# Differential attention, steps 1 to 3: one dense step issued between the scores and the transposes that follow them

## The chip, the cores and the metric

The kernel runs on one core of a Trainium2 chip. The metric is the device time of one execution in microseconds. A core has five engines that run their own instruction queues in order and meet only at semaphores: TensorE (PE, with its weight loads shown apart as PEld), VectorE (DVE), ScalarE (ACT), GpSimd (POOL), and SyncE (SP), which here issues the transfers.

## The reference, cut to what matters

The kernel computes two transformer blocks on a sequence of 1024 positions and a width of 1024, in float32. The part that the change touches is the differential attention of the second block. Eight heads, each with two maps of scores, are computed in blocks of 128 queries:

```
def diff_attention(q, k, v, g_q, g_k, lam, g_sub, lambda_init):
    qn = head_rmsnorm(q, g_q) * (HEAD_DIM_2 ** -0.5)
    kn = head_rmsnorm(k, g_k)
...
        s = jnp.einsum('bqhid,bkhid->bihqk', qblk, kn)
        s = jnp.where(allowed, s + bias, neg)
        p = jax.nn.softmax(s, axis=-1)
        a = p[:, 0] - lam * p[:, 1]
        return jnp.einsum('bhqk,bkhe->bqhe', a, vf)
...
    o = head_rmsnorm(o, g_sub) * (1.0 - lambda_init)
```

Before it, q, k and v of a head come from a product of the normalised input with a slice of w_in (z = h @ w_in). `allowed` lets a query see keys up to the end of its own chunk of 64.

## The kernel before, in words

Every dense product is made to float32 accuracy from two halves: an operand is split into a high part (HH for the activations, WH for the weights) and the remainder (HL, WL), and three products are summed in PSUM. A chunk is 128 output rows of such a product. It has eight **dense steps**, one for each 128 rows of the contraction; a step (`step`, which calls `mm3`, line 545 in the rows) is six matmuls of 512 columns, each with a weight load of 128 columns. ScalarE rounds the weights of a chunk to WH, GpSimd makes WL, and SP loads the next chunk's weights once WL is done.

The attention has eight heads j. The heads 1 to 6 run in a loop that holds two heads in its body, one for each parity of the buffers; head 0 and head 7 are written out. A head has eight **steps s** = 0 to 7, one for each block of 128 queries, and step s has s + 1 blocks of 128 keys. I call the stretch of TensorE's program that begins with scores(s) slot s. In slot s TensorE issues, in this order:

- `scores(s)` (line 885): the scores of both maps, into two pairs of PSUM banks. It waits until VectorE has read the scores of step s - 1 (`d_max`).
- `turn(s - 1, 0)` (line 866): the transposes of the weighted difference dP of step s - 1, up to four blocks, and from five blocks on `turn(s - 1, 1)` for the rest. It waits for dP (`d_a`) and until the bank with the blocks turned before has been emptied (`d_atl`).
- in slot 0 the transposes of the values (line 837), in slot 2 `output_sums` (line 844), the sums of squares of the outputs of the head before (not in head 0), in slots 4 and 6 `group_sums` (line 829), the same for the next head's q and k.
- `steps(n)`: dense steps of the next head's q, k and v, three chunks, 24 steps in all. They fill TensorE while the other engines work on the softmax. `D_STEPS = (0, 3, 3, 2, 3, 5, 3, 5)` says how many a slot has, and the larger half of them (`early`; none of them in slots 4 and 6) stands before the second group of transposes and the values. The first step of each chunk waits for `free[0]`, until the accumulator (the first two PSUM banks) is free; for a head's first dense step that is when VectorE has made dVL, the low part of the values, from it. Head 7 has no next head and no dense steps of this kind.
- `values(s - 1)` (line 661) for odd s - 1: the product of the turned differences of two steps with the values.

The other engines follow step by step. **VectorE**: two passes over the scores of step s (line 1702) add the bias, write the negated scores and find the row's minimum; then it makes the low part ATL of the turned blocks of step s - 1 (line 1395); then it waits for both exponentials, and lines 1754 to 1756 and 1391 make dP of step s. In slot 1 it makes dVL ahead of its passes; at the end of slot 2 it copies the output of two steps (line 1731) and normalises the outputs of the head before (dOT, line 1388). **ScalarE**: the high part ATH of the turned blocks of step s - 1 (line 1286), then the two exponentials of step s (lines 1304 and 1306) with their sums; in slot 2, between the two, `ln_outputs` (line 1246), the logarithm of the sums of squares that output_sums has made, and after the exponentials line 1255. Ln and exp each come with a load of their function table.

Of the kernel before, what the change touches and what calls it, by code (L numbers as in the profile page):

```python
# [121 lines left out]
def blocks_of(t, g):  # L122

    return range(4 * g, min(t + 1, 4 * g + 4))
# [23 lines left out]
def group_index(s):  # L148

    return NG * (s // ST) + (GROUPS[s % ST - 1] if s % ST else 0)  # L150


def block_kernel(nc, xt, cb, vecs, consts, mods, wst, out):
    with ExitStack() as ctx:
# [385 lines left out]
        def _(pe):  # L540
# [8 lines left out]
            def step(c, slot, pair, RH, RL, k, nk=KT, read=None):  # L549

                if k == 0:
                    pe.wait_ge(w_hi, c + 1)
                    pe.wait_ge(w_lo, c + 1)
                b = slice(k * P, (k + 1) * P)
                last = mm3(pair * S, WH[slot][:, b], WL[slot][:, b], RH, RL, k, k == 0, k == nk - 1)
                if k == nk - 1:
                    last.then_inc(chunk_done, 1)
                elif read is not None:
                    last.then_inc(read, 1)
# [92 lines left out]
            def value_sum(t, n, VH, VL):  # L652


                h, l = ATH[n], ATL[n]
                parts = [(kb, v, a) for kb in (0, t, *range(1, t)) for v, a in ((VH, h), (VH, l), (VL, h))]
                if t == 1:
                    parts = [parts[i] for i in (0, 3, 4, 5, 1, 2)]
                for i, (kb, v, a) in enumerate(parts):
                    r = 1 if kb == t else 0  # L660
                    last = pe.matmul(PS[:, OB + (2 * n + r) * P:OB + (2 * n + 2) * P], v[:, kb * P:(kb + 1) * P],
                                     a[:, (2 * kb + r) * P:(2 * kb + 2) * P], start=(i == 0), stop=(i == len(parts) - 1))
                return last

            def next_chunk(c, slot, name, k):

                if k == 0:
                    pe.wait_ge(free[0], USED["bout" if name == "y" else name][0])
                pe.wait_ge(f_lo, FILL[name] + k + 1)
                step(c, slot, 0, HH, HL, k)  # L670
# [129 lines left out]
            for g in (2, 3):  # L800
                s = (C_POOL + g) % 2
# [23 lines left out]
            def group_sums(n):  # L825

                pe.wait_ge(d_sq, n)
                for h in (0, HALF):
                    last = pe.matmul(PS[:, h:h + HALF], dBD[:, :], dSQ[:, h:h + HALF], start=True, stop=True)  # L829
                last.then_inc(d_ss, 1)  # L830

            def turn_values(j, par):

                pe.wait_ge(d_v, j + 1)
                for t in range(ST):
                    b = slice(t * P, (t + 1) * P)
                    last = pe.transpose(PS[:, b], dVR[par][:, b], IDF[:, :])
                last.then_inc(d_vt, 1)

            def output_sums(n):  # L840

                pe.wait_ge(d_sq, n)
                for h, o in enumerate(OSUM):
                    last = pe.matmul(PS[:, o:o + HALF], ONES[:, :], dSQ[:, h * HALF:(h + 1) * HALF], start=True, stop=True)
                last.then_inc(d_ss, 1)
# [8 lines left out]
            def attention_d(j, par, fill=True, first=False):  # L854


                used = 3 * j + (ud[0] + 2)

                def turn(s, g):
                    if s < 0 and first or g >= len(GROUP_BLOCKS[s % ST]):  # L860
                        return
                    pe.wait_ge(d_a, ST * j + (s + 1))
                    if not (first and s == 0 and g == 0):
                        pe.wait_ge(d_atl, NG * j + (group_index(s) + g))
                    for n, kb in enumerate(blocks_of(s % ST, g)):
                        last = pe.transpose(PS[:, TB + n * P:TB + (n + 1) * P], dP0[s % 2][:, kb * P:(kb + 1) * P], IDF[:, :])
                    last.then_inc(d_t, 1)

                def scores(s):
                    n = (s + 1) * P  # L870
                    q = slice(s * P, (s + 1) * P)
                    pe.wait_ge(free[1], ST * j + (ud[1] + s))
                    if s == 4 and not first:
                        pe.wait_ge(d_lo, j)
                    if first and s == 0:
                        pe.wait_ge(free[2], ud[2])
                    else:
                        pe.wait_ge(d_max, ST * j + s)
                    parts = ((dQH, dKH), (dQH, dKL), (dQL, dKH))
                    for i, (l, rr) in enumerate(parts):  # L880
                        for c0 in range(0, n, HALF):
                            w = min(HALF, n - c0)
                            for m in range(2):
                                rows, base = slice(m * HD, (m + 1) * HD), (1 + m) * S
                                last = pe.matmul(PS[:, base + c0:base + c0 + w], l[par][rows, q], rr[par][rows, c0:c0 + w],
                                                 start=i == 0, stop=i == 2)
                                if i == 2 and c0 + w == n:
                                    last.then_inc(d_s, 1)

                def values(s):  # L890

                    if s % 2 == 0 or s < 0 and first:
                        return
                    if not (first and s < 4):
                        pe.wait_ge(d_o, ST // 2 * j + (s + 1) // 2 - 2)
                    if s == 1:
                        pe.wait_ge(free[0], used + 1)
                    pe.wait_ge(d_atl, NG * j + group_index(s + 1))
                    v = par if s >= 0 else 1 - par
                    value_sum(s % ST, s // 2 % 2, dVH[v], dVL[v]).then_inc(d_av, 1)  # L900

                k = 0

                def steps(n):

                    nonlocal k
                    for _ in range(n if fill else 0):
                        c = k // KT
                        if k % KT == 0:
                            pe.wait_ge(free[0], used + (1 + c))  # L910
                        step(3 * j + (C_QKV2 + 3 + c), (C_QKV2 + 3 * par + 3 + c) % 2, 0, HH, HL, k % KT)
                        k += 1

                pe.wait_ge(d_split, j + 1)
                for s in range(ST):
                    scores(s)
                    turn(s - 1, 0)
                    if s == 0:
                        turn_values(j, par)
                    if s == 2 and not first:  # L920
                        output_sums(3 * j + 2)
                    if fill and s in (4, 6):
                        group_sums(3 * j + (3 if s == 4 else 4))
                    early = 0 if s in (4, 6) else (D_STEPS[s] + 1) // 2
                    steps(early)
                    if not fill and s >= 3:
                        next_chunk(C_AB, C_AB % 2, "ab", s - 3)
                    turn(s - 1, 1)
                    values(s - 1)
                    steps(D_STEPS[s] - early)  # L930
                if fill:
                    return
                turn(ST - 1, 0)
                next_chunk(C_AB, C_AB % 2, "ab", ST - 3)
                turn(ST - 1, 1)
                next_chunk(C_AB, C_AB % 2, "ab", ST - 2)
                values(ST - 1)
                pe.wait_ge(d_max, ST * KT)
                output_sums(3 * KT)

            attention_d(0, 0, first=True)
            with pe.Fori(0, (KT - 2) // 2) as i:
                for m in range(2):
                    attention_d(2 * i + (1 + m), 1 - m)
            attention_d(KT - 1, 1, fill=False)
            next_chunk(C_AB, C_AB % 2, "ab", KT - 1)
            u = USED["ab"]
# [1041 lines left out]
```

## Time and profile before

| | |
|---|---|
| time, median of 3 runs | 3137.21 us (3136.54 to 3137.8) |
| the profiled execution's own time | 3134.09 us |
| its span, first to last instruction | 3132.3 us |
| TensorE busy | 2847.5 us (91%) |
| VectorE, ScalarE, GpSimd busy | 1257.9, 1129.1, 720.7 us |
| granted clock of TensorE, mean | 0.964 of full speed |
| where the differential attention lies | 1684 to 2226 us of the span |

Busy times of different engines overlap; they don't add up to the span. The busy time of TensorE counts matmuls, which are pipelined: the end of one lies behind the start of the next. So what a piece of TensorE's work takes is read from start to start. A row of the time order gives the start, the duration, the engine, the line and the tiles (out<-in), how many instructions are merged in it, and in brackets how long the engine had been idle and what released it.

### The profile page before, as it was taken

To read this page: it belongs to the slowest core of one execution; us is meant where nothing else is said; L and a number is where in the kernel's file an instruction comes from. 1 tells how busy PE (TensorE), PEld (TensorE's weight loads), DVE (VectorE), ACT (ScalarE), POOL (GpSimd) and SP (SyncE) were. 2 spreads that over 40 slices of the span, in tenths; PEclk is the share of its full clock that TensorE was granted. 3 is DMA by queue.
4 is the path that set the end of the run, shared out by engine and by line. 5 is a ranking of instruction groups with operands and counts; after the bars stand their busy time and mean duration, and the time that the engine had idled before them with its cause. 6 is when DMAs were issued, how large, how long until landed. Compare 5 with 4: busy or idle time off the path is not lost.

```text
span 3132.3 us, 38031 instructions
## 1 busy us (share of the span) xinstructions
PE 2847.5 (91%) x13672; PEld 2283.7 (73%) x13672; DVE 1257.9 (40%) x1751; ACT 1129.1 (36%) x1585; POOL 720.7 (23%) x387
## 2 busy tenths in 40 slices
PE   5999998998888875979998898898798999999999
PEld 3888886877777764768786666665586888888887
DVE  5545433135666654370103555556442412112121
ACT  4212213225565553243215666666312312112120
POOL 0222221223444431212222111110112122222222
PEclk8999998999999986989999999998899999999999
DMA  5433322442211211102231000001331111111112
GB/s 198 133 122 115 120 68 71 170 158 78 85 57 47 86 48 45 63 32 96 101 134 37 33 29 27 34 33 55 114 114 47 41 47 47 54 47 47 47 48 100
DMA packets 62570, 236.81 MB, mean 76 GB/s; under 512 B 6944, under 2 KB 7584, under 8 KB 59936
## 3 DMA queue, kind: packets, MB, share of 16 engines
q1 hardware_dynamic: 62496, 235.88, 21.7%
q8 instruction: 40, 0.66, 0.1%
q14 instruction: 34, 0.28, 0.0%
HBM read 191.81 MB, written 44.04 MB: 75 GB/s over the span
## 4 chain that ended last, share of the span: by engine, by line
issue 69%; PE 17%; POOL 8%; DVE 4%; ACT 2%; POOLq 0%; DVEq 0%; ACTq 0%; DMA 0%; SPq 0%
PE PS L545 10%; POOL WL L1825 7%; DVE bC L1580 2%; PE PS L706 2%; PE PS L728 2%; DVE ATL L1395 2%; ACT PS L1117 1%; PE PS L691 1%; PE PS L754 1%; POOL dBIAS L1880 1%; PE PS L711 0%; ACT bB L1116 0%; PE PS L829 0%; POOLq L1872 0%; ACT ATH L1109 0%
## 5 line engine op out<-in xcount | busy, mean ns | idle before, releaser
L1825 POOL TENSOR_TENSOR WL<-WR,WH 128x1024 fp32r<-128x1024 f32 x215 | 522.0, 2428 | 2096.0 <-ACT WH L984 2090.0
L545 PE MATMUL PS<-HH,WH 128*128 128x512 f32 x2272 | 727.2, 402 | 93.7 <-issue 28.8
L545 PE MATMUL PS<-HL,WH 128*128 128x512 f32 x2272 | 713.1, 396 | 0.0
L545 PE MATMUL PS<-HH,WL 128*128 128x512 f32 x2272 | 711.3, 395 | 0.0
L545 PEld LDWEIGHTS PS<-HH,WH 128*128 128x128 f32 x2272 | 426.5, 192 | 199.1 <-issue 74.2
L545 PEld LDWEIGHTS PS<-HL,WH 128*128 128x128 f32 x2272 | 435.6, 192 | 93.5
L545 PEld LDWEIGHTS PS<-HH,WL 128*128 128x128 f32 x2272 | 434.3, 191 | 92.9
L984 ACT ACTIVATE WH<-WR 128x1024 fp32r<-128x1024 f32 x214 | 225.6, 1054 | 590.5 <-PE PS L545 413.7
L545 PE MATMUL PS<-GH,WH 128*128 128x512 f32 x768 | 236.7, 389 | 1.6 <-DVE TMP L1795 1.5
L545 PE MATMUL PS<-GH,WL 128*128 128x512 f32 x768 | 236.5, 389 | 0.0
L545 PE MATMUL PS<-GL,WH 128*128 128x512 f32 x768 | 236.4, 389 | 0.0
L1580 DVE TENSOR_TENSOR_SCAN bC<-PS,EPSC 128x256 f32<-128x256 f32 (+7 forms) x128 | 172.9, 1352 | 102.5 <-ACT PS L1117 102.3
L1853 POOL TENSOR_TENSOR bB<-bB,bC 128x256 f32<-128x256 f32 (+7 forms) x128 | 154.0, 1205 | 176.9 <-DVE bC L1580 175.8
L1395 DVE TENSOR_TENSOR ATL<-PS,ATH 128x512 fp32r<-128x512 f32 (+3 forms) x288 | 152.6, 546 | 49.2 <-ACT ATH L1286 24.7
L545 PEld LDWEIGHTS PS<-GH,WH 128*128 128x128 f32 x768 | 144.0, 188 | 32.2 <-issue 1.9
L545 PEld LDWEIGHTS PS<-GH,WL 128*128 128x128 f32 x768 | 144.2, 188 | 29.9
L545 PEld LDWEIGHTS PS<-GL,WH 128*128 128x128 f32 x768 | 144.2, 188 | 29.9
L1817 DVE TENSOR_TENSOR X<-PS,X 128x1024 f32 x32 | 39.2, 1225 | 292.2 <-PE PS L545 292.2
L691 PE MATMUL PS<-IDF,bB 128*128 128x128 f32 x576 | 99.0, 298 | 58.3 <-DVE ATL L1395 57.5
L691 PEld LDWEIGHTS PS<-IDF,bB 128*128 128x128 f32 x576 | 67.2, 148 | 82.8 <-DVE ATL L1395 52.9
L1808 DVE SCALAR_TENSOR_TENSOR TMP<-PS,TMP 128x1024 f32<-128x1024 f32 x32 | 39.2, 1224 | 207.7 <-ACT TMP L1374 207.7
L1374 ACT ACTIVATE TMP<-PS 128x1024 f32<-128x1024 f32 x32 | 32.9, 1027 | 233.4 <-PE PS L545 233.4
(226 smaller groups left out, 3504.7 us busy)
## 6 DMA issues: line engine op xcount, KB each, us to landing
WR<-wst SPq DMA_DIRECT2D x215, 512.0 KB, 3.4
TMP<-mods SPq DMA_DIRECT2D x48, 512.0 KB, 3.7
MRAW<-mods SPq DMA_DIRECT2D x16, 512.0 KB, 10.5
v_hl<-VS SPq DMA_DIRECT2D x8, 1024.0 KB, 6.3
bV<-v_hl SPq DMA_DIRECT2D x8, 1024.0 KB, 7.4
X<-xt SPq DMA_DIRECT2D x4, 1024.0 KB, 8.0
x_b<-X SPq DMA_DIRECT2D x8, 512.0 KB, 4.8
k_hi<-KSH SPq DMA_DIRECT2D x8, 512.0 KB, 4.9
```

Source lines behind the costliest of these rows:

```text
L545: last = pe.matmul(PS[:, dst0 + q:dst0 + q + HALF], l, rr[:, k * S + q:k * S + q + HALF], start=a, stop=z)
L691: last = pe.transpose(PS[:, base + n * P:base + (n + 1) * P], bB[t % 2][h][:, kb * P:(kb + 1) * P], IDF[:, :])
L706: pe.matmul(PS[:, base + c0:base + c0 + w], l[par][rows, q], rr[par][rows, c0:c0 + w], start=i == 0, stop=i == 2 and c0 + w < n)
L728: last = pe.matmul(PS[:, o + r * P:o + 2 * P], value_weights(V, kb, h), a[:, (2 * kb + r) * P:(2 * kb + 2) * P], start=i == 0 and a is ATH ...
L984: act.activation(WH[slot][:, :], WR0[:, :], ACT.Identity).then_inc(w_hi, 1)
L1374: act.activation(T[m], PAIR[s], ACT.Relu).then_inc(ff_r, 1)
L1395: return dve.tensor_tensor(dst, value, high.bitcast(F32), ALU.subtract)
L1580: dve.tensor_tensor_scan(bC[h][:, S - n:S][:, ::-1], c, EPSC[:, 0:1].broadcast_to([P, n]), 1.0, ALU.mult, ALU.bypass).then_inc(free[1 + h], 1)
L1808: dve.scalar_tensor_tensor(out=T[2 + m], in0=PAIR[s], scalar=0.0, in1=T[m], op0=ALU.max, op1=ALU.mult).then_inc(free[s], 1)
L1817: dve.tensor_tensor(x, PAIR[s], x, ALU.add).then_inc(free[s], 1)
L1825: pool.tensor_tensor(WL[slot][:, :], WR0[:, :], WH[slot][:, :].bitcast(F32), ALU.subtract).then_inc(w_lo, 1)
L1853: pool.tensor_tensor(b, b, bC[h][:, S - n + 1:S + 1], ALU.mult).then_inc(b_a, 1)
```

## The change

In slots 1, 2 and 3 of every head one dense step is issued after the scores and ahead of the transposes, and one less after them. The number of dense steps in a slot and their order stay the same. In head 7 `steps` issues nothing, and there is no change.

```
                 for s in range(ST):
                     scores(s)
+                    if s in (1, 2, 3):
+                        steps(1)
                     turn(s - 1, 0)
...
                     early = 0 if s in (4, 6) else (D_STEPS[s] + 1) // 2
-                    steps(early)
+                    steps(early - (1 if s in (1, 2, 3) else 0))
```

With `early` of 2, 2 and 1 in these slots: slot 1 goes from scores, turn(0), 2 dense steps, 1 dense step to scores, 1 dense step, turn(0), 1, 1. Slot 2 goes from scores, turn(1), output_sums, 2 dense steps, values(1), 1 dense step to scores, 1 dense step, turn(1), output_sums, 1, values(1), 1. Slot 3 goes from scores, turn(2), 1 dense step, 1 dense step to scores, 1 dense step, turn(2), 1.

## Rows read from the trace of the kernel before

**Rows 1.** The page, part 1: busy time of TensorE.
```profile
PE 2847.5 (91%) x13672; PEld 2283.7 (73%) x13672; DVE 1257.9 (40%) x1751; ACT 1129.1 (36%) x1585; POOL 720.7 (23%) x387
```

**Rows 2.** Waits of TensorE, 1752 to 2152 us: total us, times, longest us.
```profile
PE PS L866 <- DVE dP L1391: 9.3, 6, 1.6
PE PS L545 <- DVE dVL L1395: 6.1, 6, 1.0
```

**Rows 3.** Busy time by stretch: from:to, length, busy by engine, granted clock, DMA.
```profile
1688.60:1692.50 3.90, 3.90 (x10) 3.04 (x11) 2.07 (x9) 1.09 (x4) 2.10 (x1) 0.58 0.16 47
1754.00:2150.00 396.00, 357.38 (x1932) 267.13 (x1931) 226.65 (x543) 255.03 (x399) 57.63 (x24) 1.00 0.10 33
```

**Rows 4.** In order of time, TensorE, head 4: start us, duration us, what.
```profile
1960.26 0.33 PE L866 MATMUL PS<-IDF,dP 128*128 128x128 f32 x1
1961.61 0.70 PE L545 MATMUL PS<-HH,WH 128*128 128x512 f32 x2 [1.02 <-DVE dVL L1395]
...
1965.88 0.44 PE L885 MATMUL PS<-dKH,dQH 64*128 64x384 f32 x2
...
1966.60 0.44 PE L866 MATMUL PS<-IDF,dP 128*128 128x128 f32 x2
1966.87 1.88 PE L844 MATMUL PS<-dSQ,ONES 128*128 128x512 f32 x4
...
1973.51 0.50 PE L885 MATMUL PS<-dKH,dQH 64*128 64x512 f32 x2
...
1974.40 0.55 PE L866 MATMUL PS<-IDF,dP 128*128 128x128 f32 x3
...
1977.63 0.56 PE L885 MATMUL PS<-dKH,dQH 64*128 64x512 f32 x4
...
1980.43 0.65 PE L866 MATMUL PS<-IDF,dP 128*128 128x128 f32 x4 [1.55 <-DVE dP L1391]
```

**Rows 5.** In order of time, ScalarE and VectorE, head 4.
```profile
1962.10 0.51 ACT L1304 ACTIVATE dP<-dP,SM 128x256 f32<-128x256 f32 x1 [0.53 <-DVE SM L1702]
...
1964.07 0.48 DVE L1391 SCALAR_TENSOR_TENSOR dP<-dP,SM,dP 128x256 f32<-128x256 f32 x1
...
1967.07 0.38 ACT L1286 ACTIVATE ATH<-PS 128x256 fp32r<-128x256 f32 x1 [3.88 <-PE PS L866]
...
1967.47 1.28 ACT L1246 ACT_TABLE_LOAD   x1
...
1968.79 1.27 ACT L1246 ACTIVATE dSQ<-PS,EPSC 128x512 f32<-128x512 f32 x2
...
1970.08 1.28 ACT L1304 ACT_TABLE_LOAD   x1
...
1971.37 0.62 ACT L1304 ACTIVATE dP<-dP,SM 128x384 f32<-128x384 f32 x1
...
1973.62 0.62 DVE L1391 SCALAR_TENSOR_TENSOR dP<-dP,SM,dP 128x384 f32<-128x384 f32 x1
...
1974.49 1.28 DVE L1388 SCALAR_TENSOR_TENSOR dOT<-dOT,GS,dRS 128x1024 f32<-128x1024 f32 x1
...
1975.69 0.69 DVE L1702 CUSTOM_DVE_ANT_0 dP<-PS,dBIAS 128x512 f32<-128x512 f32 x1
...
1977.03 0.72 ACT L1304 ACTIVATE dP<-dP,SM 128x512 f32<-128x512 f32 x1 [1.55 <-DVE SM L1702]
...
1979.55 0.75 DVE L1391 SCALAR_TENSOR_TENSOR dP<-dP,SM,dP 128x512 f32<-128x512 f32 x1
```

**Rows 6.** In order of time, TensorE and ScalarE, head 0.
```profile
1688.60 0.73 PE L545 MATMUL PS<-HH,WH 128*128 128x512 f32 x2 [1.06 <-DVE dVL L1395]
...
1694.51 0.44 PE L885 MATMUL PS<-dKH,dQH 64*128 64x384 f32 x2
...
1702.83 0.72 ACT L1304 ACTIVATE dP<-dP,SM 128x512 f32<-128x512 f32 x1 [0.41 <-DVE SM L1702]
...
1706.17 0.65 PE L866 MATMUL PS<-IDF,dP 128*128 128x128 f32 x4 [0.34 <-DVE dP L1391]
```

More of the change, by code:

```diff
@@ L916, in attention_d @@
                     scores(s)
+                    if s in (1, 2, 3):
+                        steps(1)
                     turn(s - 1, 0)
@@ L924, in attention_d @@
                     early = 0 if s in (4, 6) else (D_STEPS[s] + 1) // 2
-                    steps(early)
+                    steps(early - (1 if s in (1, 2, 3) else 0))
                     if not fill and s >= 3:
```

## The prediction, made before the changed kernel was run

> **What bounds the kernel now.** Read the page first. TensorE is busy for 2847.5 us of the span of 3132.3 us [rows 1], so the end of the kernel is set by TensorE's work and by the holes in it, and an edit that only reorders that work can pay or cost only through the holes. Read next the waits of TensorE over the six middle heads of the differential attention (heads 1 to 6, 1752 to 2152 us). Two lines matter to this change: 9.3 us in six waits ahead of the transposes of step 3 (line 866, for the weighted difference dP of line 1391), and 6.1 us in six waits ahead of a head's first dense step (line 545, for dVL, which frees the accumulator) [rows 2]. Six heads, six equal waits: the heads repeat one pattern, so one head can be read for all. The granted clock over them is 1.00, the 2.4 GHz level; the stretch of head 0 in which its first dense steps run is at 0.58, a mixture of the two levels [rows 3].
>
> Third, read head 4 in order of time. I write turn(n) for the transposes that TensorE makes of step n's dP, and scores(n) for its score matmuls. In the row order of TensorE [rows 4], turn(0) starts at 1960.26, TensorE then idles 1.02 us for dVL, three dense steps run from 1961.61 to scores(2) at 1965.88, turn(1) follows at 1966.60 and output_sums at 1966.87; scores(3) at 1973.51, turn(2) at 1974.40, scores(4) at 1977.63, and then TensorE stands until turn(3) at 1980.43, the wait of 1.55 us of rows 2.
>
> What ends that last wait is found by walking back on ScalarE and VectorE [rows 5]. dP of step 3 (1979.55, 0.75 us) follows exp(3) at 1977.03; that waited for the minimum of step 3, whose passes over the scores start on VectorE at 1975.69; they stand behind the normalisation of dOT (1974.49, 1.28 us), that behind dP of step 2 (1973.62), that behind exp(2) at 1971.37. Ahead of exp(2) ScalarE has a table load, the two Ln passes (1968.79) and another table load (1967.47), and ahead of these the eviction ATH of turn(1), at 1967.07, before which ScalarE idled 3.88 us for turn(1) itself. From turn(1) to turn(3) there is thus one unbroken chain through ScalarE and VectorE, 1980.43 - 1966.60 = 13.83 us, none of whose links waits for dense work. TensorE has less than that to do in the meantime, which is the 1.55 us hole.
>
> **The change part by part.** Nothing is added or removed: 24 dense steps a head, in the same order, with the same waits inside them. The moved step's six matmuls and six weight loads and its waits (for the accumulator at step 0 of a chunk, for w_hi and w_lo) are all on TensorE; no DMA moves. SP's load of the next weights and the split on GpSimd hang on chunk_done, and the eighth dense step, which sets it, stays the last of slot 3; neither queue is passed by anything. One step now stands ahead of turn(0), turn(1) and turn(2) in heads 0 to 6; head 7 has no dense steps.
>
> The price of a step: three of them fill 1961.61 to 1965.88, 4.27 / 3 = 1.42 us each. At the lower clock of head 0 the same three fill 1688.60 to 1694.51 [rows 6], 5.91 / 3 = 1.97 us each. The ends for a step are thus 1.42 and 1.97; in the six heads at clock 1.00 I take 1.42.
>
> Slot 1, turn(0). The moved step is the head's first, the one that waits for dVL. It can't start before 1961.61 wherever it stands, so the hole stays, and turn(0), which ran inside it, is now queued behind the wait: 1961.61 + 1.42 = 1963.0 instead of 1960.26. Behind turn(0) wait its eviction and then exp(1) on ScalarE (1962.10 before, now about 1963.6) and dP of step 1 on VectorE (end 1964.07 + 0.48 = 1964.6, now 1966.1). Who waits for that dP is turn(1), which comes after 1968, so this lateness is covered by 2 us of TensorE's own work; without that cover it would cost 1.5 us a head. What does show is that turn(0) leaves the cover of the wait. Between nothing and its own 0.33 us, I take half of what the two transposes of turn(1) hold TensorE (1966.60 to 1966.87, 0.27), 0.13 us.
>
> Slot 2, turn(1). A step of 1.42 us goes between scores(2) and turn(1), whose dP is ready. Turn(1) moves by 1.42 + 0.13 = 1.55 us, to 1968.15, and output_sums, queued behind it, moves with it. This is the head of the chain above, and ScalarE was idle there. Every link moves by 1.55: dP of step 2 ends at about 1975.8, the passes of step 3 start at 1977.2, exp(3) at 1978.6, turn(3) at 1980.43 + 1.55 = 1981.98.
>
> The Trainium skill bears on the length of this chain. Rows 5 show a table load of 1.28 us both ahead of Ln and ahead of the exp that follows. "ScalarE: Activation LUTs", section "Table sets: the hidden batching unit", says that one set, natural_log_exp_and_others, holds both functions and that ln followed by exp needs one load. By that page the chain could be two loads shorter, the wait of 1.55 us would be mostly gone before the change, and the change would then cost only some 0.5 us a head, about 3141 us in all. The trace doesn't agree, this program does switch tables each time, and the measurement decides.
>
> Slot 3, turn(2). Scores(3) starts at 1973.6, ends its work in about 0.9 us (1973.51 to 1974.40), and the moved step fills 1974.5 to 1975.9, just as long as dP of step 2 is late. So turn(2) goes at about 1975.9 without a wait of its own; its eviction is over by 1977, before exp(3) needs ScalarE at 1978.6. This edit costs nothing, because slot 2's delay covers it; alone it would push the eviction to about 1976.9, still ahead of exp(3) at 1977.03. One step is left in slot 3, and TensorE reaches scores(4) at about 1977.7. There a new wait stands: scores(4) needs both passes of step 3 done, which was so at 1977.0 and now is so at about 1978.6. That is about 1.0 us of hole, and after scores(4) another of 2.0 us ahead of turn(3) where there were 1.55.
>
> From turn(3) on all three engines are late by the same 1.55 us, and the rest of the head is unchanged, so nothing gives it back. The six heads cost 6 x 1.55 = 9.3 us.
>
> Head 0 has no output_sums, no Ln pair and no dOT normalisation in slot 2. Its exp(3) waited 0.41 us after the eviction of turn(2), and turn(3) followed after a hole of 0.34 [rows 6]. Turn(2) moves by 1.55, the eviction with it, exp(3) by 1.55 - 0.41 = 1.1, and turn(3) by 1.1. Ends for head 0: 0 and 2.1 (a step at the lower clock). Sum: 9.3 + 1.1 = 10.4 us. The profiled execution took 3134.1 us (span 3132.3), so it would take 3144.5. It lies 3.1 us below the median of the runs, and I put the sum on the median: 3137.2 + 10.4 = 3147.6 us.
>
> **Rivals.** (1) Not slower. If turn(1) were not what releases ScalarE (if the load and the Ln were waiting for something of their own that ends 1.5 us after turn(1)), the chain would stay where it is and only TensorE's own small terms count: 7 x 0.13 us for turn(0) uncovered, less about 0.1 us a head of the 0.36 us that turn(2) waited. That is nothing: 3137.2 us. It decides from the point where ScalarE has 1.55 us of slack behind turn(1). For it: turn(1) and output_sums stand so close that the row of the Ln alone doesn't tell which it followed. Against it: both move together, and ScalarE's row shows 3.88 us idle up to turn(1) and then no gap to exp(2).
>
> (2) The clock falls. Each head gets 1.5 us more of holes within 6 us, and if the granted clock then fell once a head to 1.2 GHz as in head 0's first steps, where holes of about 1 us came shortly before, each head would pay 5.91 - 4.27 = 1.64 us more: 6 x 1.64 = 9.8, so 3157.4 us. Against it: the same heads hold holes of 1.0 and 1.55 us now and keep 1.00 throughout [rows 2, 3]. The Trainium skill, "TensorE: Matmul & The Clock Gate", section "HAM oscillation — how this bites in real kernels", says that waits between bursts of matmuls put the clock back, burst after burst. By that rule this rival would be right; the trace so far agrees only for head 0.
>
> (3) Faster. The step stands in for waits: the 0.36 us ahead of turn(2) vanishes six times and nothing else moves, which gives 3135.0 us. To be faster by more than a measurement tells, the 1.55 us ahead of turn(3) would have to go too, and no moved step stands between scores(4) and turn(3).
>
> **How the numbers follow.** A measurement of this kernel can tell about 0.2%, 6.3 us. Chances: the forecast (3145 to 3150) 0.68; part of the shift only, in some heads or with slack that I don't see (3140 to 3145) 0.07; the clock rival, wholly or in some heads (3150 to 3157.4) 0.10; not slower 0.12; faster 0.03, of which most lies within 0.2%. Slower by over 0.2%, from 3143.5 up: 0.68 + 0.10 + 0.04 = 0.82; within 0.2%: 0.16; faster by over 0.2%: 0.02. The range takes in the forecast, the partial case and the lower half of the clock rival: 3140 to 3154 us.
>
> **What would show it.** In the trace of the changed kernel, over heads 1 to 6: head to head about 1.55 us more; ScalarE's idle time before the eviction of turn(1) longer, about 3.9 us or more, and from there to exp(2) the same 4.3 us; a new line of waits of scores on the passes of line 1702, six of about 1 us; the six waits ahead of turn(3) near 2.0 us; the 1.0 us wait for dVL unchanged; clock 1.00. Turn(3) coming 13.8 us after turn(1) as before is the test of the chain. I am wrong if that distance shrinks to about 12.3 us (rival 1), or if the granted clock of these heads is below 1.00 (rival 2).

## The result, and the profile after

The changed kernel takes 3158.1 us (median; 3157.3 to 3159.8) against 3136.9 us before in the same comparison: slower by 21.3 us, ratio 1.0071 with a 95% interval of 1.0057 to 1.0086. The profiled execution took 3159.8 us, its span 3158.0, that is 25.7 us over the span of before. The prediction was 3147.6 us, range 3140 to 3154. The direction was right, the size half of what came.

Start with the page of the changed kernel, part 1, the row that answers to [rows 1]:

```profile
PE 2866.2 (91%) x13672; PEld 2298.5 (73%) x13672; DVE 1257.5 (40%) x1751; ACT 1129.0 (36%) x1585; POOL 719.3 (23%) x387
```

The number of matmuls is the same, and TensorE is busy 18.7 us longer with them. A step that only waits would leave the busy time alone; so part of the loss isn't waiting but slower matmuls. The other engines are busy as long as before.

The waits of TensorE over heads 1 to 6 of the changed kernel, 1750 to 2170 us (total us, times, longest us), beside [rows 2]:

```profile
PE PS L866 <- DVE dP L1393: 12.8, 6, 2.1
...
PE PS L545 <- DVE dVL L1397: 7.2, 6, 1.3
PE PS L885 <- DVE SM L1704: 3.9, 6, 0.6
```

The six waits ahead of turn(3) went from 1.55 to 2.1 us, and a new line of six appeared, scores(4) for the passes of step 3, 0.65 us each. Together they are 3.9 + 12.8 - 9.3 = 7.4 us more. The wait for dVL was 1.0 and is 1.28 in most heads, because turn(0) no longer stands inside it. That is another 1.1 us over the six heads, and not unchanged as the prediction had it.

Now one head in order of time, TensorE and ScalarE, head 4 of the changed kernel. Its rows answer to [rows 4, 5]:

```profile
1973.20 0.70 PE L545 MATMUL PS<-HH,WH 128*128 128x512 f32 x2 [1.28 <-DVE dVL L1397]
...
1979.84 0.38 PE L866 MATMUL PS<-IDF,dP 128*128 128x128 f32 x2
1980.06 1.88 PE L844 MATMUL PS<-dSQ,ONES 128*128 128x512 f32 x4
1980.26 0.38 ACT L1288 ACTIVATE ATH<-PS 128x256 fp32r<-128x256 f32 x1 [3.96 <-PE PS L866]
...
1984.56 0.62 ACT L1306 ACTIVATE dP<-dP,SM 128x384 f32<-128x384 f32 x1
...
1987.71 0.49 PE L866 MATMUL PS<-IDF,dP 128*128 128x128 f32 x3
...
1990.22 0.72 ACT L1306 ACTIVATE dP<-dP,SM 128x512 f32<-128x512 f32 x1 [1.49 <-DVE SM L1704]
1990.24 0.56 PE L885 MATMUL PS<-dKH,dQH 64*128 64x512 f32 x4 [0.65 <-DVE SM L1704]
...
1993.62 0.65 PE L866 MATMUL PS<-IDF,dP 128*128 128x128 f32 x4 [2.14 <-DVE dP L1393]
```

From the first dense step to turn(1) it is 1979.84 - 1973.20 = 6.64 us, 1.65 more than the 4.99 of before. ScalarE idles 3.96 us up to turn(1), exp(2) follows the eviction by 4.30 us as before, and from turn(1) to turn(3) it is 13.78 us against 13.83. The chain is the one described, unchanged in length and only started later.

The turn(3) of heads 1 to 6 in the changed kernel, and then those of the kernel before (that of head 4 stands in [rows 4]), give the length of a head:

```profile
1778.12 0.65 PE L866 MATMUL PS<-IDF,dP 128*128 128x128 f32 x4 [2.14 <-DVE dP L1393]
1850.26 0.65 PE L866 MATMUL PS<-IDF,dP 128*128 128x128 f32 x4 [2.13 <-DVE dP L1393]
1924.15 0.66 PE L866 MATMUL PS<-IDF,dP 128*128 128x128 f32 x4 [2.14 <-DVE dP L1393]
1993.62 0.65 PE L866 MATMUL PS<-IDF,dP 128*128 128x128 f32 x4 [2.14 <-DVE dP L1393]
2067.41 1.11 PE L866 MATMUL PS<-IDF,dP 128*128 128x128 f32 x4 [2.14 <-DVE dP L1393]
2140.64 0.65 PE L866 MATMUL PS<-IDF,dP 128*128 128x128 f32 x4 [2.14 <-DVE dP L1393]
```

```profile
1775.99 0.65 PE L866 MATMUL PS<-IDF,dP 128*128 128x128 f32 x4 [1.55 <-DVE dP L1391]
1843.89 0.65 PE L866 MATMUL PS<-IDF,dP 128*128 128x128 f32 x4 [1.55 <-DVE dP L1391]
1912.58 0.65 PE L866 MATMUL PS<-IDF,dP 128*128 128x128 f32 x4 [1.55 <-DVE dP L1391]
...
2049.08 0.65 PE L866 MATMUL PS<-IDF,dP 128*128 128x128 f32 x4 [1.56 <-DVE dP L1391]
2116.93 0.65 PE L866 MATMUL PS<-IDF,dP 128*128 128x128 f32 x4 [1.55 <-DVE dP L1391]
```

Before, heads take 67.9 and 68.7 us in turn (the loop's body holds two). After, they take 72.1, 73.9, 69.5, 73.8 and 73.2. The third of these is longer by 1.6 us, which is the chain. The others are longer by 4.2 to 5.4 us. What is different about them is the clock. Stretches of the changed kernel (from:to, length, busy by engine, granted clock, DMA), beside [rows 3]:

```profile
1754.00:2170.00 416.00, 369.43 (x1909) 276.91 (x1908) 223.10 (x535) 253.62 (x398) 58.91 (x24) 0.95 0.09 31
1779.00:1782.40 3.40, 3.40 (x11) 2.03 (x9) 1.35 (x3) 2.77 (x3) 3.32 (x2) 0.57 0.00 0
1895.00:1902.00 7.00, 5.54 (x26) 5.35 (x26) 1.75 (x6) 3.21 (x7) 2.37 (x1) 0.54 0.04 8
1904.00:1973.00 69.00, 61.11 (x332) 45.58 (x331) 38.96 (x93) 43.86 (x69) 9.85 (x4) 1.00 0.07 23
```

The mean clock of these heads fell from 1.00 to 0.95. The 1.2 GHz level is granted in nine stretches: right after turn(3) in heads 1, 2, 4, 5 and 6 (the second row is the first of them), and in slot 0 of heads 2, 3, 5 and 6 (the third row). Between the dense steps of head 3 and those of head 4, the last row, there is none, and that is the head that is only 1.6 us longer.

So the 25.7 us divide as follows, from first dense step to turn(3) and from there to the next head's first dense step. The chain: 6 x 1.6 = 9.6 us, and 1.05 in head 0 (17.57 us from the first to the second before, 18.62 after). The clock: 2.6, 3.6, 0.0, 3.6 and 3.8 us between heads, and 2.0 from turn(3) of head 6 to the end of the span (1.3 of it by turn(1) of head 7), 15.6 us. One fall that the kernel before had in slot 0 of head 1 is gone, 2.0 us back, and the profiled execution reached head 0 1.4 us later, which is ahead of the first changed instruction. These are two single executions. The medians lie 21.3 us apart; if the chain costs the same 10.6 us in every execution, 10.7 us are left for the clock.

### The profile page after: what moved, and what is told of

The parts are those of the page before. It is cut to its first block, busy times and chain, and to the rows that moved or that the text cites. A ratio compares the mean times of both kernels' runs of the same rounds, so it can differ in the third digit from the quotient of the medians.

```text
span 3158.0 us, 38031 instructions
## 1 busy us (share of the span) xinstructions
PE 2866.2 (91%) x13672; PEld 2298.5 (73%) x13672; DVE 1257.5 (40%) x1751; ACT 1129.0 (36%) x1585; POOL 719.3 (23%) x387
## 4 chain that ended last, share of the span: by engine, by line
issue 66%; PE 19%; POOL 7%; DVE 4%; ACT 2%; POOLq 0%; DVEq 0%; ACTq 0%; DMA 0%; SPq 0%
PE PS L545 13%; POOL WL L1827 6%; DVE bC L1582 2%; PE PS L706 2%; PE PS L728 2%; DVE ATL L1397 2%; ACT PS L1119 1%; PE PS L691 1%; PE PS L754 1%; POOL dBIAS L1882 1%; PE PS L711 0%; ACT bB L1118 0%; PE PS L598 0%; PE PS L829 0%; ACT ATH L1111 0%
```

## The experiments

Two causes had to be told apart and shown: which of the moved steps starts the chain, and what makes the clock fall. For the clock there were two theories. By the one, it falls after the longer holes around scores(4). By the other, holes that were there all along (those of slot 0 among them) make it fall or not according to when they come, and in longer heads they come at other times. Both can be true together. The runs below stand in that order. Each ratio is against runs of the kernel before on the same chip.

**One slot at a time.** Slot 2 alone:

```
-                    if s in (1, 2, 3):
+                    if s in (2,):
                         steps(1)
...
-                    steps(early - (1 if s in (1, 2, 3) else 0))
+                    steps(early - (1 if s in (2,) else 0))
```

> The step is moved ahead of the transposes in slot 2 alone. Chain theory (turn(1) releases the chain through ScalarE and VectorE that ends in turn(3)): turn(3) comes about 1.4 us later in each of heads 1 to 6, the distance from turn(1) to turn(3) stays 13.8 us, and the time rises by about 6 x 1.4 = 8.5 us plus 1 us in head 0, to about 3146 us if the clock stays at its upper level in these heads, and by some 10 us more, to about 3157 us, if the clock falls as it does in the changed kernel. Rival (the three moved steps share the cost): a third of the 21 us, about 3144 us. Rival (turn(1) has slack): 3137 us.

Measured: 3148.75 us, ratio 1.0043 (1.0027 to 1.0060), 13.4 us more. The mean clock of heads 1 to 6 is 0.98, with five falls, three in slot 0 (of heads 1, 3 and 6) and two after turn(3). Its waits of TensorE over the six heads:

```profile
PE PS L866 <- DVE dP L1393: 17.1, 12, 1.7
```

Twelve waits for dP, not six: turn(2) now waits too, 1.2 us, since its dP is late and no step has been moved ahead of it. From first dense step to turn(3) it is 20.3 us against 18.8, in each of the six heads; the head without a fall is 1.5 us longer. One moved step makes the whole chain late, at 6 x 1.45 = 8.7 us. In head 0, where 1 us was expected, nothing changed (17.62 us against 17.57). The rest of the 13.4 us is lower clock, less of it than in the changed kernel, so the number lies between the 3146 and the 3157 of the chain theory.

Slots 1 and 3, `if s in (1, 3)` in both places:

> The step is moved in slots 1 and 3 and left where it was in slot 2. Chain theory: turn(1) comes only 0.13 us later, exp(3) still waits for the passes on VectorE, so 6 x 0.1 = under 1 us in the six heads, and 0 to 1 us in head 0, where exp(3) follows turn(2) more closely: 3137 to 3139 us, clock 1.00 in heads 1 to 6. Rival (each moved step costs): two thirds of the 21 us, about 3151 us.

Measured: 3136.3 us, ratio 1.0005 (0.9995 to 1.0014), no change in the median. Six waits ahead of turn(3) of 1.49 us, clock:

```profile
1754.00:2145.00 391.00, 351.39 (x1897) 262.34 (x1897) 222.70 (x536) 253.19 (x398) 58.14 (x24) 1.00 0.10 33
```

So the chain's cost in the six heads comes with the step of slot 2. The other two add 0.15 us a head, and the 1.05 us of head 0 is theirs: its hole ahead of turn(3) is 1.18 us here and stayed at 0.34 with slot 2 alone. Together that is 8.7 + 0.9 + 1.0 = 10.6 us, the chain's part of the changed kernel.

The clock's part is not settled by these two. The changed kernel costs 8 us more than slot 2 alone, and the ten executions of slots 1 and 3 fall in two groups: five of 3130.7 to 3133.8 us at a mean clock of 0.965 to 0.966, the profiled one among them, and five of 3138.7 to 3140.7 us at 0.961 to 0.963. The same program keeps the clock up in one execution and loses some of it in another; no trace shows where it was lost in the second group.

**Take the Ln out of the chain.** In this run and the next, output_sums is issued in slot 1, after turn(0), and ScalarE takes the logarithm after the exponentials of step 1. On the kernel before:

```
-                    if s == 2 and not first:
+                    if s == 1 and not first:
                         output_sums(3 * j + 2)
...
-                    if s == 2 and not first:
-                        ln_outputs(3 * j + 2)
...
+                    if s == 1 and not first:
+                        ln_outputs(3 * j + 2)
                     if s == 2 and not first:
                         exp_d(3 * j + 2, d_lo, j)
```

> The kernel before, but output_sums is issued in slot 1 right after turn(0), where TensorE waits for dVL, and ScalarE takes the logarithm after the exponentials of step 1, where it is idle for 3.9 us until turn(1). Chain theory: the two table loads and the Ln passes leave the chain from turn(1) to turn(3), exp(3) is then released by the scores of step 3, and the hole ahead of turn(3) shrinks from 1.55 to about 0.5 us: 6 x 1.1 = 6.5 us less, about 3129 us with the clock as before. If the length of a head decides whether the holes of slot 0 lower the clock, heads that are 1.1 us shorter can lose it again: up to 6 x 1.5 = 9 us on top. If the chain does not run through the Ln, 3136 us as before.

Measured: 3131.2 us, ratio 0.9987 (0.9978 to 0.9997), 4.5 us less. Waits of TensorE over the six heads:

```profile
PE PS L844 <- ACT dSQ L1316: 5.3, 6, 0.9
PE PS L866 <- DVE dP L1391: 3.8, 6, 0.6
```

The hole ahead of turn(3) fell from 1.55 to 0.64 us, close to the 0.5 expected, and from turn(1) to turn(3) it is 11.24 us (1969.01 to 1980.25 in head 4), 2.6 less than before. Output_sums now waits 0.9 us for the squares, and the wait for dVL is gone from the list. Every second head also has one fall of the clock in slot 0, where before only one head had. A head without one is 0.7 us shorter, one with it 0.7 us longer.

The same on the changed kernel:

> The changed kernel with output_sums and the logarithm in slot 1 as in the run before. Chain theory: a late turn(1) no longer delays turn(3) through the Ln; what is left is that turn(2) is a step late and exp(3) then follows it, about 1.1 us a head against the run before, so a hole of about 1.6 us ahead of turn(3) as in the kernel before, and 3131 to 3137 us at a clock of 1.00, up to 9 us more if the clock falls in slot 0. If the moved steps cost by themselves and not by the Ln chain, 3150 us or more.

Measured: 3142.2 us, ratio 1.0020 (1.0010 to 1.0030). That is 16 us under the 3158 of the changed kernel (from another chip, but the kernel before took the same there, 3136.9 and 3135.7). But it is still 11.0 us over the run before, which has the same base without the moved steps: moving the pair makes both kernels faster and takes about half of the change's cost, not all of it. A head without a fall is 68.6 us long, where the run before has 67.15: 1.4 us more for the moved steps, hardly less than the 1.6 us with the pair in the chain.

The expectation had the mechanism wrong here. It let exp(3) hang on the late turn(2). The trace of head 4 shows otherwise:

```profile
1973.33 0.38 PE L866 MATMUL PS<-IDF,dP 128*128 128x128 f32 x2
...
1975.44 0.61 ACT L1304 ACTIVATE dP<-dP,SM 128x384 f32<-128x384 f32 x1
...
1980.01 0.49 ACT L1288 ACTIVATE ATH<-PS 128x384 fp32r<-128x384 f32 x1 [2.31 <-PE PS L866]
...
1981.10 0.72 ACT L1304 ACTIVATE dP<-dP,SM 128x512 f32<-128x512 f32 x1 [0.60 <-DVE SM L1704]
...
1984.51 0.66 PE L866 MATMUL PS<-IDF,dP 128*128 128x128 f32 x4 [1.97 <-DVE dP L1393]
```

The eviction of turn(2) (1980.01) is over 0.60 us before exp(3), which is released by VectorE's passes, as in the run before (0.63 us there). Turn(3) follows turn(1) by 11.18 us, against 11.24 in the run before. It is the old chain from turn(1), through one table load and exp(2), with the Ln pair out of it and 2.6 us shorter, and a late turn(1) still makes all of it late. The Ln pair made the chain long; the change doesn't need it to cost. The medians' 11 us don't divide further: the profiled execution, at 3137.7 us, is one of the three fastest of ten, and seven took 3141.8 to 3142.7. Its clock falls in slot 0 of head 3 and after turn(3) of head 6.

**Fill the hole ahead of turn(3).** In the changed kernel, ahead of the waits of turn(3), in heads 1 to 6. The result of these matmuls is overwritten:

```
+                    if s % ST == 3 and g == 0 and fill and not first:
+                        pe.wait_ge(d_atl, NG * j + (group_index(s) + g))
+                        for _ in range(6):
+                            pe.matmul(PS[:, TB:TB + HALF], IDR[:, :], HH[:, 0:HALF], start=True, stop=True)
```

> The changed kernel with six additional matmuls of 512 columns in heads 1 to 6 whose result nobody reads, issued between scores(4) and the wait of turn(3), where TensorE stands idle for about 2.1 us. They take about 1.4 us there, so they delay nothing, and the chain is as late as in the changed kernel. Theory (the lower clock of the heads comes from the longer holes around scores(4)): the clock no longer falls after turn(3), the cost of the chain alone is left, and the time falls from 3158 to about 3147 to 3150 us. Rival (the clock falls because the heads are longer and meet the gate at other points of time; the holes of slot 0, which the change did not touch, do it as much): the falls after turn(3) go or not, but those in slot 0 stay, and the time is 3152 to 3158 us.

Measured: 3150.0 us (3146.0 to 3150.8), ratio 1.0043 (1.0026 to 1.0060). The wait ahead of turn(3) is 0.47 us instead of 2.14 and turn(3) is hardly earlier, 20.3 us after the first dense step where it was 20.4. The number lies with the first theory, and the trace gives each its share: the falls after turn(3) are all gone (first row, the place of the first of them), those of slot 0 stay, three of them (second and third row).

```profile
1777.00:1790.00 13.00, 12.92 (x67) 9.53 (x66) 8.24 (x18) 10.15 (x15) 5.10 (x2) 1.00 0.12 41
1820.00:1826.00 6.00, 5.09 (x30) 4.70 (x30) 2.25 (x7) 2.63 (x8) 2.37 (x1) 0.72 0.01 1
2031.00:2040.00 9.00, 6.77 (x34) 6.33 (x34) 3.00 (x10) 3.29 (x8) 2.38 (x1) 0.64 0.09 23
```

**Make heads longer without a hole.** The kernel before, with seven such matmuls behind the waits of turn(4), in slot 5, where TensorE is busy throughout:

```
                         pe.wait_ge(d_atl, NG * j + (group_index(s) + g))
+                    if s % ST == 4 and g == 0 and fill and not first:
+                        for _ in range(7):
+                            pe.matmul(PS[:, TB:TB + HALF], IDR[:, :], HH[:, 0:HALF], start=True, stop=True)
```

> The kernel before with seven additional matmuls of 512 columns in heads 1 to 6 whose result nobody reads, issued ahead of the transposes of step 4 (slot 5), where TensorE is busy without a hole. They make each head about 1.6 us longer by busy time, about as much as the chain did, and add no idle time. Theory (the clock falls because of the added idle time): clock 1.00 in these heads as before, and 6 x 1.6 = 9.6 us more, about 3147 us. Rival (the length of a head decides whether its holes of slot 0 make the clock fall): falls of the clock in slot 0 of some heads, as in the changed kernel, and 3149 to 3155 us.

Measured: 3147.4 us, ratio 1.0045 (1.0028 to 1.0061), 12.0 us more. The number lies with the first theory (3147) and below the rival's range; it is the trace that decides. Its waits are those of before to the tenth of a microsecond, six of 1.55 ahead of turn(3) and six of 1.0 for dVL. And yet the clock now falls in slot 0 of heads 1 to 5. The time from turn(3) of head 5 to that of head 6, with no fall in it, is 1.7 us longer than before (69.55 against 67.85), the others are 3.2 us longer, so a fall costs 1.5 us. That makes 6 x 1.7 + 4 x 1.5 = 16 us for the six heads, since one fall was there before; the profiled execution had gained 2.9 us ahead of head 0, and the medians show 12.0. Slot 0 of head 3, in this run and then in the kernel before:

```profile
1889.00:1895.00 6.00, 4.50 (x25) 4.36 (x24) 1.71 (x5) 3.21 (x7) 2.36 (x1) 0.72 0.00 0
```

```profile
1889.00:1895.00 6.00, 4.98 (x37) 4.33 (x38) 3.29 (x11) 3.59 (x7) 2.39 (x1) 1.00 0.12 29
```

No idle time was added, only length. So the second theory is right for slot 0: holes that are the same lower the clock or don't. That it is the moment at which they come that decides fits both this run and the two groups of executions above, but no run shows it directly.

**Fill the holes of slot 0 as well.** Three runs: the changed kernel with all holes filled, the longer heads with the holes of slot 0 filled, and as a control the kernel before with the holes of slot 0 filled and nothing else. The edit (the bank is empty until step 4; in the first run the last loop stands ahead of the moved step and has four):

```
+                    if fill and not first and s == 0:
+                        for _ in range(4):
+                            pe.matmul(PS[:, S + HALF:2 * S], IDR[:, :], HH[:, 0:HALF], start=True, stop=True)
                     turn(s - 1, 1)
+                    if fill and not first and s == 0:
+                        for _ in range(5):
+                            pe.matmul(PS[:, S + HALF:2 * S], IDR[:, :], HH[:, 0:HALF], start=True, stop=True)
                     values(s - 1)
...
+                    if fill and not first and s == 1:
+                        for _ in range(3):
+                            pe.matmul(PS[:, S + HALF:2 * S], IDR[:, :], HH[:, 0:HALF], start=True, stop=True)
```

> The changed kernel with matmuls of 512 columns that nobody reads in all its larger holes of heads 1 to 6: six ahead of turn(3), four and five ahead of the second transposes and the values of slot 0, four ahead of the wait for dVL. They are issued where TensorE waits anyway. If all the rest of the cost, 21 us less the chain's 10, is the lower clock and all its falls follow from these holes, the clock is 1.00 in heads 1 to 6 and the time is 3145 to 3148 us, and each head is 1.6 us longer than before. If the clock falls for another reason, it stays at 3150 us as with the one hole filled.

Measured: 3145.7 us (3141.2 to 3147.6), ratio 1.0030 (1.0020 to 1.0040), 10.0 us over before. Clock of heads 1 to 6:

```profile
1754.00:2155.00 401.00, 379.57 (x2012) 281.08 (x2012) 223.24 (x536) 252.98 (x396) 59.14 (x24) 1.00 0.09 32
```

> The kernel before with the seven additional matmuls in slot 5 and with its holes of slot 0 filled in the same way (four, five and three matmuls). With the holes of slot 0 open, seven additional matmuls gave five falls of the clock there. If those falls need both the longer head and the holes, none is left: clock 1.00, each head 1.6 us longer than before, 3144 to 3146 us. If the longer head alone does it, the falls stay and so do 3147 to 3154 us.

Measured: 3144.5 us, ratio 1.0029 (1.0017 to 1.0040), clock 1.00 in the same stretch, and the heads 69.8 and 70.2 to 70.3 us in turn. The median is 3 us lower against its base than with the holes open, which the two intervals don't separate; that the falls are gone is read from the trace.

> The control of the filled runs: the kernel before with its holes of slot 0 filled by matmuls that nobody reads (four, five, three) and nothing else. They stand where TensorE waits, and the clock was 1.00 in these heads already, so nothing is to be won: 3133 to 3137 us, head to head 68.3 us, clock 1.00. If the filling itself costs or gains, it shows here, and the filled runs have to be read against this one.

Measured: 3136.0 us, ratio 1.0005 (0.9995 to 1.0014). Filling neither costs nor gains where the clock was up. No fall was expected, and there was one in the profiled execution, after turn(3) of head 2, whose hole is the 1.55 us of before.

```profile
1845.00:1849.00 4.00, 3.10 (x7) 1.87 (x8) 3.06 (x7) 3.66 (x4) 2.14 (x1) 0.63 0.00 0
```

With the holes filled, the late chain alone is left, 10.0 us, and longer heads cost their length. The lower clock needs a hole, and holes of the kernel before are enough for it, in slot 0 and ahead of turn(3); its 1.00 was no margin.

But the first theory isn't refuted either. Count the falls after turn(3) over the six heads of every profiled execution. With the 2.14 us hole of the changed kernel there are five in six heads, with the 1.97 us of the run with moved steps and sums in slot 1 one in six. With holes of 1.49 to 1.68 us (seven runs, the two with longer heads and the faster version below among them) there are three in 42 heads, and with 0.47 to 0.64 us none in 18. Longer heads with the old 1.55 us hole had no such fall. So the new falls after turn(3) go with the widened holes, and those of slot 0 with holes that the change didn't touch.

**A version that beats both.** On the kernel before with the sums in slot 1: the values are turned into the two banks that are empty until step 4, which frees the accumulator, so two dense steps can be issued in slot 0, in its holes.

```
-D_STEPS = (0, 3, 3, 2, 3, 5, 3, 5)
+D_STEPS = (2, 2, 2, 2, 3, 5, 3, 5)
...
-                    last = pe.transpose(PS[:, b], dVR[par][:, b], IDF[:, :])
+                    o = OSUM[t // 4] + t % 4 * P
+                    last = pe.transpose(PS[:, o:o + P], dVR[par][:, b], IDF[:, :])
...
-                        if k % KT == 0:
+                        if k % KT == 0 and c:
                             pe.wait_ge(free[0], used + (1 + c))
...
                     turn(s - 1, 1)
+                    if s == 0:
+                        steps(D_STEPS[0] - early)
+                        values(s - 1)
+                        continue
                     values(s - 1)
+                    if s == 1 and not first:
+                        pe.wait_ge(free[0], used + 1)
+                        output_sums(3 * j + 2)
```

ScalarE and VectorE make dVH and dVL from the two banks in two instructions each instead of one.

> A version meant to beat both kernels, built on the kernel before: the values are turned into the upper banks of the two score pairs, which are empty until step 4, so the accumulator is free and a head's first two dense steps can be issued in slot 0, in the holes ahead of the second transposes and of the values (D_STEPS 2, 2, 2, 2, 3, 5, 3, 5); output_sums and the logarithm stand in slot 1. Theory (only holes of TensorE can be won): of the 4.5 us of holes a head between turn(7) and the first dense step about 3.8 go, of the 1.55 ahead of turn(3) about 1: 3.8 to 4.8 us a head, six heads, and head 0 a little: 3105 to 3113 us if the clock stays up. Rival (dVL and the outputs come later on VectorE because the steps delay the values, and new holes open in slots 1 to 3, where fewer steps are left): 3120 to 3130 us.

Measured: 3107.8 us (3106.1 to 3110.9), ratio 0.9918 (0.9901 to 0.9934), 26.6 us less than before and some 50 less than the changed kernel. Waits of TensorE over heads 1 to 6:

```profile
PE PS L867 <- DVE dP L1399: 12.0, 12, 1.7
PE PS L661 <- DVE ATL L1403: 5.6, 6, 0.9
PE PS L867 <- DVE ATL L1403: 5.1, 11, 0.7
```

The wait for dVL is gone, and those of slot 0 are down to 1.8 us a head; a head is about 65.1 us long. The hole ahead of turn(3) is back at 1.66 us, where about 1 us of it was to go, because fewer steps are left in slots 1 to 3: part of the rival's mechanism is there at less than its price. So a head won 3.1 us and not 3.8 to 4.8; the sum came out in its range because head 0 won 3.3 us, where a little was expected, and the stretch behind turn(3) of head 6 another 4.4, which wasn't in the sum. No fall of the clock is seen in heads 1 to 6.

## Why the prediction was right or wrong

**The chain, the main term: right.** Predicted 1.55 us a head, found 1.6; turn(1) to turn(3) 13.8 us as before; 1.1 us in head 0, found 1.05; the sum 10.4 us, and the changed kernel with its holes filled, where the chain is the only cost left, measured 10.0 us. Slots 1 and 3 at next to nothing in the six heads was right as well, 0.15 us a head by a run of their own. In head 0 the 1.05 us is the price of those two alone: moving the step of slot 2 cost nothing there.

**The holes: near in sum, off in place.** 1.0 us ahead of scores(4) and 2.0 ahead of turn(3) were predicted; 0.65 and 2.14 came, and 0.26 us more ahead of the first dense step, for which none was predicted. The share of scores(4) was smaller, since TensorE reached it later than reckoned: 16.4 us after the first dense step (1990.24 - 0.65 - 1973.20), where 16.1 were expected. A moved step that follows scores takes 1.49 us (1978.35 to 1979.84 in head 4), not 1.42, and there are two of them. The 0.36 us ahead of turn(2) that rivals 1 and 3 count on is idle time of the weight loads; the matmul rows of [rows 4] have no wait there.

**The clock: wrong, and it is half the result.** It was a rival with a chance of 0.10 and a price of 9.8 us, and the forecast took the clock at 1.00. The step that failed is the argument against that rival: "the same heads hold holes of 1.0 and 1.55 us now and keep 1.00 throughout [rows 2, 3]". That row says that the clock stood up to these holes at the times at which they came. I read it as room for more. The runs show that there was none: heads made longer by busy work, with every hole as before, lost the clock in five of six slots 0. The same reading hid part of the place. The rival counted one fall a head, at the new holes; five came there, after turn(3), and four more in slot 0, whose holes were there before, and three of the nine were twice as long, so that a head paid up to 3.8 us where the rival had 1.64. Its total of 3157.4 us is within 1 us of the measured 3158.1, by luck: it had fewer falls, at a higher price than the 1.3 to 1.6 us of a short one. The kernel before did show such a fall itself, in slot 0 of head 1 (1750.00 to 1752.00 us at a clock of 0.67), just ahead of the stretch I took for [rows 3]. Taking that head in would have told that holes of slot 0 can lower the clock.

**The rule beside rival 2.** The Trainium skill, "TensorE: Matmul & The Clock Gate", section "HAM oscillation — how this bites in real kernels", describes waits for transfers between bursts of matmuls that put the clock back at every burst. Those waits are longer than any hole here (2.14 us at most), so the prediction read more into the page than it states when it said that by its rule the rival would be right. In this case's traces the clock does go back after shorter holes, nine times in the changed kernel. The same holes with the clock at 1.00 in other heads and runs show that holes of this size do so only at some times.

**The table loads.** The Trainium skill ("ScalarE: Activation LUTs", section "Table sets: the hidden batching unit") would have let Ln and exp share one load, and the prediction followed the trace instead, which has a load ahead of each. The changed kernel has them too, and the time by the shared set, about 3141 us, didn't come. Taking the pair out of the chain made it 2.6 us shorter and shrank the hole ahead of turn(3) from 1.55 to 0.64 us. It didn't bring the cost of the moved steps down to the 0.5 us a head of that estimate: 1.4 us were left. That isn't a clean test of it, since output_sums left the stretch between turn(1) and turn(3) as well.

**The range.** Its upper end was set at half the clock rival, 3154. Nothing in the rows had said that the rival would come by half; once its mechanism was on the list, with one fall a head assumed and not read from a row, the range had to hold the whole of it.

## What to carry to other kernels

Before work is put ahead of an instruction, walk back from the next hole and ask whether that instruction starts the chain that ends it: here a dense step that filled nothing made the transposes, and with them two table loads, a logarithm and a softmax, late by its own length. Holes are best filled with work at the place where they stand (the values turned into idle banks, two steps into slot 0), not by moving work about in front of a late chain. And where TensorE has regular holes of one to two microseconds, don't count on a granted clock of 1.00 until a run with a slightly different timing keeps it, and price the loss in every change's range.

## What the runs showed of the hardware

- The granted clock of TensorE falls to the 1.2 GHz level after holes of at most 2.14 us between work, or not, with the same holes. In slot 0 (holes of 0.7, 0.5, 1.5 and 1.0 us within 10 us) it fell in one of six heads before, in five of six when each head was 1.7 us longer by busy time, and in none of 18 with the holes filled. After turn(3) it fell in five of six heads where the hole ahead of it was 2.14 us, in three of 42 at 1.49 to 1.68 us and in none of 18 at 0.47 to 0.64 us. What else decides the moment is not settled by these runs.
- One short stretch of low clock (3.4 us in the rows) cost 1.3 to 1.6 us of a head's time, and up to two stretches came in one head.
- The same program can differ by 5 to 10 us between executions with the mean clock: slots 1 and 3 took 3130.7 to 3133.8 us at 0.965 to 0.966 and 3138.7 to 3140.7 us at 0.961 to 0.963. One profile shows only one of these.
- Matmuls whose result nobody reads, issued in holes where TensorE waits anyway, cost nothing measurable (ratio 1.0005, 0.9995 to 1.0014) and the clock stayed up with them: 3145.7 us against 3158.1 for the changed kernel, and, within the noise, 3144.5 against 3147.4 for the longer heads (these pairs ran on different chips, on which the kernel before took 3135.3 to 3136.9).
